# Attention's norms moved into the block of the delta rule, attention one slot behind it, and the delta queries' norm folded into the output norm

## The reference, cut to what matters

```python
def gated_delta_rule(q, k, v, ...):            # 4 heads of 128
    q = l2norm(q) * (Dh ** -0.5)               # one factor per position and head
    k = l2norm(k)
    ...                                         # chunked scan with state S
    o = qg_i @ S + qk_i @ v_new                 # both terms are linear in q
o_a = rms_norm(o_a, out_norm) * silu(z_a)

def sliding_window_attention(q, k, v, q_gain, k_gain, sinks, band_bias):
    q = rms_norm(q, q_gain) * (Dh ** -0.5)      # 8 heads of 64
    k = rms_norm(k, k_gain)                     # 2 key heads of 64
    s = q @ k_window + band_bias                # 128 keys for each 64 queries
    p = softmax of s with a sink; o = p @ v_window
o_b = o_b * silu(z_b)
```

## Time and profile before

| | us |
|---|---|
| median of 3 runs | 1367.37 (1365.17 to 1368.5) |
| the profiled execution | 1369.78 |
| its span | 1368.0 |

### The profile page before, as it was taken

One profiled execution on the slowest core, in us unless ns is written; L12 is line 12 of the kernel. 1 busy time (PEld: TensorE's weight loads), 2 busy tenths in 40 slices (PEclk: granted clock), 3 DMA queues, 4 the chain that ended last, 5 costly groups with the idle time before them and its releaser, 6 DMA issues. The chain is left out here.

```text
span 1368.0 us, 20296 instructions
## 1 busy us (share of the span) xinstructions
PE 1235.3 (90%) x8326; PEld 1013.8 (74%) x8326; DVE 855.9 (63%) x1204; ACT 485.6 (35%) x844; POOL 248.6 (18%) x139
## 2 busy tenths in 40 slices
PE   5999999999968989998999999999972679899898
PEld 4677777888737877877878888887641467788787
DVE  6266873760146768227986765695989869465821
ACT  6234246232145665115233221233744322332500
POOL 3222222221003330014222121222320410000000
PEclk9999999999979999999999999999985679999999
DMA  6322121330040014411232251621200000030432
GB/s 205 48 47 58 32 54 47 110 106 32 19 160 1 2 48 167 157 62 36 100 106 91 78 135 48 200 54 47 77 31 1 1 1 1 3 124 1 170 92 108
DMA packets 117556, 97.77 MB, mean 71 GB/s; under 512 B 37016, under 2 KB 102680, under 8 KB 117336
## 3 DMA queue, kind: packets, MB, share of 16 engines
q1 hardware_dynamic: 103832, 77.46, 18.7%
q10 hardware_dynamic: 13632, 19.01, 4.3%
HBM read 70.24 MB, written 24.51 MB: 69 GB/s over the span
## 5 line engine op out<-in xcount | busy, mean ns | idle before, releaser
L179 PE MATMUL banks<-xt_lo,w_hi 128*128 128x512 f32 x816 | 323.4, 396 | 5.3 <-PEq L205 4.1
L180 PE MATMUL banks<-xt_hi,w_lo 128*128 128x512 f32 x816 | 319.7, 392 | 0.0
L181 PE MATMUL banks<-xt_hi,w_hi 128*128 128x512 f32 x816 | 319.6, 392 | 0.0
L537 POOL TENSOR_TENSOR w_lo<-features,w_hi 128x1024 fp32r<-128x1024 f32 x54 | 144.0, 2667 | 490.5 <-ACT w_hi L547 490.4
L179 PEld LDWEIGHTS banks<-xt_lo,w_hi 128*128 128x128 f32 x816 | 154.5, 189 | 40.9 <-issue 7.4
L181 PEld LDWEIGHTS banks<-xt_hi,w_hi 128*128 128x128 f32 x816 | 154.4, 189 | 33.0
L180 PEld LDWEIGHTS banks<-xt_hi,w_lo 128*128 128x128 f32 x816 | 154.7, 190 | 31.4
L596 ACT ACTIVATE temporaries<-banks 128x1024 f32<-128x1024 f32 x47 | 56.1, 1193 | 307.4 <-PE banks L181 297.1
L547 ACT ACTIVATE w_hi<-features 128x1024 fp32r<-128x1024 f32 x54 | 56.8, 1053 | 2.5 <-PEq L205 1.9
L179 PE MATMUL banks<-xt_lo,eout_mh 128*128 128x512 f32 x128 | 50.9, 398 | 5.7 <-DVE xt_lo L1739 4.6
L2720 DVE COPY_PREDICATED features<-constants,banks 128x384 f32<-128x384 int32 x64 | 33.7, 580 | 33.9 <-PE banks L2641 33.6
(11 more groups left out here) (534 smaller groups left out, 2473.4 us busy)
## 6 DMA issues: line engine op xcount, KB each, us to landing
features<-in_even_w_in SPq DMA_DIRECT2D x26, 512.0 KB, 4.0
features<-in_odd_w_in SPq DMA_DIRECT2D x25, 512.0 KB, 4.4
features<-in_x SPq DMA_DIRECT2D x8, 512.0 KB, 7.7
even_gates<-temporaries ACTq DMA_DIRECT2D x8, 512.0 KB, 2.7
features<-even_gates SPq DMA_DIRECT2D x8, 512.0 KB, 8.9
features<-in_even_w_out SPq DMA_DIRECT2D x8, 512.0 KB, 3.5
temporaries<-in_x SPq DMA_DIRECT2D x8, 512.0 KB, 5.0
h_between_layers<-features SPq DMA_DIRECT2D x8, 512.0 KB, 2.9
```

Of the source, the lines that this page charges most:

```text
L179: nc.tensor.matmul(out, w[0], x[1], start=start, stop=False)
L180: nc.tensor.matmul(out, w[1], x[0], start=False, stop=False)
L181: return nc.tensor.matmul(out, w[0], x[0], start=False, stop=stop)
L537: nc.gpsimd.tensor_tensor(wl[n % 2], wr[n % NW], wh[n % 2].bitcast(F32), ALU.subtract).then_inc(low, 1)
```

## The change

- `norm_blocks` goes, and its block with it. `swa_norms` takes its place as a further program of the joint block, with due numbers from -30: the same work for five tiles only (4 `qb`, then `kb`), spread from the key tile on, through two pairs of banks instead of three.
- The four delta query tiles are no longer normed. Their squares are made (ScalarE, due -5; the third and the fourth wait for the sums of the first and the second), summed on TensorE (due -2.5, behind chunk 0's preparation) and copied to `co.q_squares` (VectorE, due -2). GpSimd's first scaling of the queries, in place, waits for the four squares.
- `delta_norm` adds one VectorE instruction (due 7.5) that joins the sums of squares with 128 x 128 x 1e-6 x `q_squares`; the root waits for it, with an epsilon of its own.
- All due numbers of `swa_attend` from its value turning on are 10 larger (`late`): step n shares its slot with chunk n+1. The sinks' DMAs (ScalarE's queue, -10) and GpSimd's memsets (-10) stay. It waits for `key_normed`, `all_normed`, `value_in`, `gates_in` and `q_kept`. SyncE issues the bias DMAs ahead of the key moves.
- The clearing of the 89 semaphores is due at -20 on GpSimd in the joint block.

```diff
-def norm_blocks(co, tag, items, params, fetch=(), ahead=(), late=None, expand=None):
+def swa_norms(co, queries, key, gains, loads, later):
...
+    items = [(x, gains[0]) for x in queries] + [(key, gains[1])]
...
+    order = [N - 1] + list(range(N - 1))
+    delta_q = co.at(A_F[0], (HG, T))
+    q_sq = [co.at(at, (T,)) for at in (A_T + 2048, A_BIG + 14400)]
...
+    def scalar(act):
+        yield -30
+        for n, (x, _) in enumerate(items):
...
+            nc.scalar.activation(sq[n % 3], x, ACT.Square).then_inc(squared, 1)
+        yield -28
+        act.wait_ge(summed, N)
+        nc.scalar.activation(rows, co.ps[:, 4, 0:Q], ACT.Sqrt, bias=eps, scale=scale).then_inc(rooted, 1)
+        yield -26
+        act.wait_ge(inverted, 1)
+        for q, (_, of) in enumerate(quarters):
+            nc.scalar.activation(high[:, of], rows, ACT.Copy, scale=own_quarter[:, q:q + 1]).then_inc(high_r, 1)
+        yield -5
+        act.wait_ge(low_r, 4)
+        for h in range(HG):
+            if h >= 2:
+                act.wait_ge(q_summed, h - 1)
+            nc.scalar.activation(q_sq[h % 2], delta_q[:, h, :], ACT.Square).then_inc(q_squared, 1)
+
+    def tensor(pe):
+        yield -30
...
+        for i, n in enumerate(order):
+            yield -5 + 0.2 * i
+            if i == 0:
+                pe.wait_ge(paired, 1)
+                pe.wait_ge(low_r, 4)
+            if i >= 2:
+                pe.wait_ge(normed, i - 1)
+            for h in range(2):
+                out = co.ps[:, 4 + 2 * (i % 2) + h, :]
+                nc.tensor.matmul(out, pairs[:, n, :], low[:, hs[h]], start=True, stop=False)
+                last = nc.tensor.matmul(out, pairs[:, n, :], high[:, hs[h]], start=False, stop=True)
+            last.then_inc(spread, 1)
+        yield -2.5
+        pe.wait_ge(normed, N - 1)
+        for h in range(HG):
+            pe.wait_ge(q_squared, h + 1)
+            for own, of in quarters:
+                last = nc.tensor.matmul(co.ps[own, 6, 0:Q], co.at(A_CST + C_SUM + R - 1 - h, (R,)), q_sq[h % 2][:, of], start=h == 0, stop=h == HG - 1)
+            last.then_inc(q_summed, 1)
+
+    def vector(dve):
+        yield -30
+        by_head_of(co, co.gc_by_head, co.gc_rows).then_inc(expanded, 1)
...
+        for i, n in enumerate(order):
+            yield -5 + 0.2 * i
...
+        yield -2
+        dve.wait_ge(q_summed, HG)
+        nc.vector.tensor_copy(co.q_squares, co.ps[:, 6, 0:Q]).then_inc(q_kept, 1)
...
 def gdn_state(co, expanded, q_squared):
...
+            if c == 0:
+                pool.wait_ge(*q_squared)
             nc.gpsimd.tensor_tensor(q[:, :, ct], q[:, :, ct], grow[c % 2], ALU.mult).then_inc(q_scaled, 1)
...
 def swa_attend(co, sinks, zb, ahead, norms, late):
...
     def tensor(pe):
-        yield -9
+        yield late - 9
         pe.wait_ge(padded, 1)
+        pe.wait_ge(*norms["value_in"])
+        pe.wait_ge(*norms["all_normed"])
+        pe.wait_ge(*norms["q_kept"])
...
             if n >= 1:
-                yield 10 * n + 1
+                yield late + 10 * n + 1
...
 def delta_norm(co, x, gain, gate):
...
-        act.wait_ge(summed, N)
-        nc.scalar.activation(rows, co.ps[:, 6, 0:Q], ACT.Sqrt, bias=eps, scale=scale).then_inc(rooted, 1)
+        act.wait_ge(joined, 1)
+        nc.scalar.activation(rows, rows, ACT.Sqrt, bias=co.at(co.eps_at[HEAD * RMS_EPS * L2_EPS], (1,)), scale=1.0 / HEAD).then_inc(rooted, 1)
...
+        yield 7.5
+        dve.wait_ge(summed, N)
+        nc.vector.scalar_tensor_tensor(rows, co.q_squares, HEAD * HEAD * RMS_EPS, co.ps[:, 6, 0:Q], ALU.mult, ALU.add).then_inc(joined, 1)
         yield 9
...
-    norm_blocks(co, "eq", [(x_, 64, qn, None) for x_ in qb] + [(kb, 64, kn, None)] + [(x_, 128, 1.0, None) for x_ in q], 0, late=(kb, kvb[0]), expand=(co.gc_by_head, co.gc_rows),
-                fetch=[(vb, kvb[1])] + [(zb[b], zg[WB + b]) for b in range(WB)] + [(za[b], zg[b]) for b in range(WB)])
...
-    side_by_side(co, swa_attend(co, a["swa_sinks"][0], co.at(A_F[6], (WB, T)), w_ahead), gdn_state(co))
+    cleared = clearing(co, at=-20)
+    norms = swa_norms(co, qb, kb, (qn, kn), [(kb, kvb[0]), (vb, kvb[1])] + [(zb[b], zg[WB + b]) for b in range(WB)], [(za[b], zg[b]) for b in range(WB)])
+    side_by_side(co, cleared, norms, swa_attend(co, a["swa_sinks"][0], co.at(A_F[6], (WB, T)), w_ahead, norms, 10), gdn_state(co, norms["expanded"], norms["q_squared"]))
```

More of the change, by code:

```diff
@@ L688, in norm_blocks @@
[L688 to L708, removed]
-            act.wait_ge(summed, N)
[L710 to L751, removed]
-                dve.wait_ge(high_r, q + 1)
-                nc.vector.scalar_tensor_tensor(low[:, of], rows, own_quarter[:, q:q + 1], high[:, of].bitcast(F32), ALU.mult, ALU.subtract).then_inc(low_r, 1)
-            for n, (x, group, gain, gate) in enumerate(items):
-                dve.wait_ge(spread, n + 1)
-                if gate is not None:
-                    dve.wait_ge(gated, gates.index(n) + 1)
-                v = x.rearrange("p (h t) -> p h t", h=2)
-                nc.vector.scalar_tensor_tensor(v, v, gain, co.ps[:, 2 + 2 * (n % 3):4 + 2 * (n % 3), :], ALU.mult, ALU.mult).then_inc(normed, 1)
@@ L760, in norm_blocks, with sync @@
-    co.release(old)
+    order = [N - 1] + list(range(N - 1))
+    delta_q = co.at(A_F[0], (HG, T))
+    q_sq = [co.at(at, (T,)) for at in (A_T + 2048, A_BIG + 14400)]
+    def sync(sp):
+        yield -30
+        sp.dma_start(*loads[0]).then_inc(key_in, 16)
+        sp.dma_start(*loads[1]).then_inc(value_in, 16)
+        for load in loads[2:]:
+            sp.dma_start(*load).then_inc(gates_in, 16)
+        for load in later:
+            sp.dma_start(*load).then_inc(other_in, 16)
+        yield 200
+        sp.wait_ge(gates_in, 16 * len(loads[2:]))
+        sp.wait_ge(other_in, 16 * len(later))
@@ L1382, in swa_views, with swa_attend @@
     return kd, vw, bias, bias0
-def swa_attend(co, sinks, zb, ahead):
+def swa_attend(co, sinks, zb, ahead, norms, late):
     nc = co.nc
@@ L1480, in vector @@
         link = Chain(dve, dch)
-        yield -9
+        yield late - 9
+        dve.wait_ge(*norms["key_normed"])
         for h in range(2):
@@ L1492, in vector @@
             if n >= 1:
-                yield 10 * n + 1
+                yield late + 10 * n + 1
                 dve.wait_ge(mixed, n)
+                if n == 1:
+                    dve.wait_ge(*norms["gates_in"])
                 z = zb[:, :, C * 64 * (n - 1):C * 64 * n].rearrange("p b (c t) -> p b c t", c=C)
```

78 lines of the change are left out of this document (51 added, 27 removed).

## The result

| | before | after |
|---|---|---|
| median of 5 runs each, us | 1365.67 (1365.1 to 1368.5) | 1359.94 (1359.32 to 1360.4) |
| ratio | | 0.9949, 95% interval 0.9938 to 0.9961 |
| span of the profiled execution | 1368.0, and 1364.6 in a second profile | 1358.1 |

The change takes 0.4 to 0.5% off: the two medians differ by 5.7 us, and their quotient is 0.9958, while the ratio of the table is the recorded estimate with its interval. Where an execution starts the block varies with no difference in the code: the same code of after started it at 369.70 and, profiled again, at 372.33.

A forecast was written before the change was run, and what follows sets the result against it. Ahead of the delta rule's first product, a chain through one engine at a time bounds it; in the pattern's slots, TensorE. -17.5 + 0.5 + 10.5 + 0 = -6.5 us gives median 1360.9, range 1357.9 to 1364.4.

The forecast's parts named there:

- Part 1: Norms ahead of the root: four squares fewer, so the chain starts 3.78 us earlier and low parts end at 384.28.
- Part 2: From the split to chunk 0's first product: it starts at 397.2 instead of 414.72, a gain of 17.5 us.
- Part 3: Slot 0 without attention: takes 11.8 us, bounds 10.5 and 14.4.
- Part 4: Slots between: 14.38, 12.92, then four of 11.32; first to last chunk's product 84.4 us against 83.9, cost 0.5.
- Part 5: Block's end, last slot to last gate: 20.3 us instead of 9.8, cost 10.5 us; bounds 8.9 and 13.
- Part 6: Output norm: the added VectorE instruction starts the root about 1.1 us later, but TensorE's projection covers it; cost 0.
- Everything behind moved by the same amount: Expected profile sign: block's end near 502 instead of 508.4, and all later code shifted equally.
- Half clock: Rival: clock stays half through new prologue and slot 0, turning -6.5 us into +4.6, median 1372.0; chance 7%.
- The ends cost more: Rival: slot 0 takes 14.4 us and the end 24.2, sum 0.0, median 1367.4; chance 11%.
- GpSimd late: Rival: 89 clears ahead of GpSimd's first decay mask take up to 25.4 us; +1.4, median 1368.8; chance 7%.
- A better clock: Rival: slot 2 keeps clock 1.00 (-1.6 us), the end is at its low bound (-1.4); median 1357.9; chance 12%.

The follow-up runs named there:

- e4_four_buffers: The whole change with four buffers instead of two for the delta queries' squares; median 1357.93 us, ratio 0.9938 to the kernel before.
- the filler's run: The whole change plus 9 and 11 useless matmuls in TensorE's two waits at the end; median 1360.51 us, ratio 0.9948 to the kernel before.
- the fold alone: Kernel before with only the delta queries' norms folded into the output norm; norm block kept, attention not behind; median 1355.21 us, ratio 0.9919.
- The delays: The whole change with the output norm's joined step repeated 4 or 8 more times, each waiting for the last; medians 1361.27 and 1364.13 us.
- e2_no_lag: The whole change without attention's numbers 10 later, norms' numbers 10 earlier; step n and chunk n share a slot; median 1358.59 us, ratio 0.9944.
- e8_early_turning_filler: The whole change with three square buffers, value turning moved into the root's wait, and useless matmuls in the end's gaps; median 1354.96 us, ratio 0.9910.
- e7_early_turning: The whole change with three square buffers and the value turning and its copy moved into the root's wait; median 1355.46 us, ratio 0.9913.

## Why the prediction was right

The mechanism held, term by term below. That the time came within 1 us of the forecast is partly luck. The block did 1.1 better than the 6.5 forecast, and behind it 1.1 was lost, 0.2 in the output norm and 0.9 in code that is the same in both kernels; and the forecast started from a median of 1367.37 of three runs, where five gave 1365.67, so that by the medians the change is worth 5.7 us and not 6.5.

- **Part 1** held: the low parts end 10.81 after the block's start; forecast 10.83.
- **Part 2**: the first product at +23.13, forecast +23.75, a gain of 18.07 instead of 17.5. The string of the sums was as costed (3.33 from 389.50 to the first product, forecast 3.4), and `e4_four_buffers` confirms that it holds up the first product, with 1.66. What was 0.55 too long was the way to it, and nearly all of that is the second half of the preparation: it begins 18.37 after the block's start (the forecast had the last spread end at 18.45) and takes 1.43, where the forecast went from 391.9 to 393.8. Its own terms, 0.6 and 1.06, make 1.66 and not 1.9.
- **Part 3**: slot 0 at 11.30, forecast 11.8. The turning took 1.91 of the 2.0, and TensorE waited 0.43, not 0.6, behind the values' copy. The remaining 0.2 to 0.3 was counted twice: the pattern's slot of 11.32 holds 0.29 of idle time of its own (11.03 busy), to which the 0.6 was added, while slot 0 has 0.43 in all (10.87 busy of 11.30).
- **Part 4** held to the tenth, with 14.38, 12.88 and 11.31. With slot 0 at 11.30 the slots cost 0.0, not 0.5.
- **Part 5** held: 20.28, forecast 20.3. ScalarE's first exponential of step 7 came 7.01 after the slot's start (forecast 7.0), the product 11.46 after it, and the clock took 1.3 by the filler's run; the 0.7 put down for it was too little and the chain at the full clock, 18.94 against the 19.6 of the forecast, too long. Two errors of 0.6 cancel here, so that the sum came out to the hundredth is luck.
- **Part 6**: the first multiplication starts 20.77 after the block's end, 20.57 before the change. The root did wait 0.89 for the joined step; 0.2 instead of 0. In the fold alone it is 1.2, and there VectorE waits for TensorE. The joined step isn't the reason: TensorE's sums, which lie ahead of it, already start 10.9 after the block's end, against 9.7 before. Of the projection's matmuls of 512 columns ahead of them, the first 13 took 0.63 or more in the fold, against 7 before; in full clock one takes 0.39. Why the half clock lasted longer there was not shown.
- **"Everything behind moved by the same amount"** was wrong. The spans differ by 6.5, with 7.4 at the first multiplication of the output norm, and 0.9 is lost behind it. The delays show that such a residue needs no cause in the changed code.
- **The rivals.** *Half clock*: slot 0 at 1.00, refuted. *The ends cost more*: 11.30 and 20.28, refuted. *GpSimd late*: all 89 clears were done 6.6 us into the block, refuted; the 9.41 of the earlier trace rows was an idle time spent waiting for ScalarE, a bound and no price. *A better clock* did not occur in after (slot 2 kept its 0.87), but a slot with a clock of 1.00 in its place occurred in the fold, in `e2_no_lag` and in `e8_early_turning_filler`.

What the prediction left out matters more for an engineer than its number. It summed the change against the kernel before and never asked what each part was worth alone. The fold alone gives 9.0 in the block, 7.5 by the shorter chain and 1.57 by the clock of slot 1. Against the fold the early norms with the lag bring the first product another 10.57 earlier and cost 10.49 more at the end; the extra slot of 11.3 replaces one of the pattern. So they give 0.1, and slot 2's lower clock takes 1.56, which makes the 7.6 of the whole change. Part 5's price was right and stood in the text; that it ate all that the lag had brought didn't.

## What to carry to other kernels

Cost each part of a compound change alone: here the part that removed work (four norms) gave in the block all that the whole change gave, and the part that overlapped two chains gave back at the end what it won at the start. A program put one slot behind another pays its own whole last chain, uncovered; measure that chain before moving it, and fill it (the value turning in the root's wait with a third buffer, and something for TensorE in the last gaps, took some 4.5 us more out of this block, and 1.6 came with the clock of one slot). Compare stages from their own starts, and don't read a difference of 1 us between totals as an effect.

## What the runs showed of the hardware

- The same instructions in the same order had a granted clock of 0.87 in one kernel and 1.00 in another (slot 2 of `e7_early_turning` and `e8_early_turning_filler`), 1.6 us apart. The Trainium skill (TensorE: Matmul & The Clock Gate, Part 1: The HAM clock gate) says that the number of matmuls at the lower clock changes from run to run with the phase at the kernel's start. The two slots would fit such a dependence in the middle of a kernel; no run here shows it.
- In single profiles, a delay of 1.56 us shrank to 0.38 and one of 3.61 grew to 6.94 over 760 us of unchanged code.
- 89 semaphore clears on GpSimd took less than 6.6 us together, under 0.08 us each (from the block's start to GpSimd's first fill at 376.31 in after).
